# Row weights copied two blocks ahead, and the gather five blocks ahead asked for in front of a block's add

## The reference, cut to what matters

```python
top_i, top_w = route(h2, w_router, router_bias)          # 8 of 64 experts per token, and 8 weights
# assignments sorted by expert, each expert's rows padded to blocks of 128 rows
def block(args):
    tok, e = args
    return swiglu(h_pad[tok], w_gate[e], w_up[e], w_down[e])   # (silu(x@Wg) * (x@Wu)) @ Wd, 1024 -> 256 -> 1024
out = lax.map(block, (row_tok.reshape(n_blocks, 128), blk_exp))
out = out.reshape(n_rows, D) * row_w[:, None]
ffn = segment_sum(out, row_tok, num_segments=T + 1)[:T] + swiglu(h2, w_sh_gate, w_sh_up, w_sh_down)
x = x + g2 * ffn                                          # then a final RMSNorm
```

## Time and profile before

| | |
|---|---|
| median of 3 runs | 2043.7 us |
| the profiled execution's own time | 2044.4 us |
| its span | 2042.8 us |
| granted TensorE clock, mean of the span | 0.974 |
| PE, PEld, DVE, ACT, POOL busy | 93%, 75%, 57%, 47%, 19% |
| DMA, all queues | 399.63 MB, mean 196 GB/s |
| expert stage (first to last L2130 group) | 1084.85 to 1990.42 us |

### The profile page before, as it was taken

One profiled execution on the slowest core, in us unless ns is written; L12 is line 12 of the kernel. 1 busy time (PEld: TensorE's weight loads), 2 busy tenths in 40 slices (PEclk: granted clock), 3 DMA queues, 4 the chain that ended last, 5 costly groups with the idle time before them and its releaser, 6 DMA issues. The chain is left out here.

```text
span 2042.8 us, 37459 instructions
## 1 busy us (share of the span) xinstructions
PE 1904.9 (93%) x10449; PEld 1527.9 (75%) x10450; DVE 1159.4 (57%) x1715; ACT 967.4 (47%) x1395; POOL 385.4 (19%) x335
## 2 busy tenths in 40 slices
PE   4999999899899999988789999999999999999995
PEld 3999999899788666765547777777777777777772
DVE  4213401166438334555426777777777777777775
ACT  5110111244213222211246777777777777777773
POOL 0110100111111000000112223232233222323330
PEclk9999999899899999999889999999999999999998
DMA  7211321111343666325058997998998889898964
GB/s 261 74 48 45 115 60 31 31 64 62 134 143 123 230 217 220 134 94 197 1 205 275 304 350 205 324 313 285 336 312 273 268 271 308 234 347 263 298 193 176
DMA packets 181813, 399.63 MB, mean 196 GB/s; under 512 B 22137, under 2 KB 86897, under 8 KB 181758
## 3 DMA queue, kind: packets, MB, share of 16 engines
q1 hardware_dynamic: 149166, 312.16, 42.8%
q0 software_dynamic: 31392, 82.49, 15.7%
q10 hardware_dynamic: 1200, 4.26, 0.6%
HBM read 350.16 MB, written 80.64 MB: 211 GB/s over the span
## 5 line engine op out<-in xcount | busy, mean ns | idle before, releaser
L2214 DVE TENSOR_TENSOR wexp_lo<-wexp,wexp_hi 128x2048 fp32r<-128x2048 f32 x189 | 432.5, 2289 | 92.3 <-ACT wexp_hi L2156 70.8
L2156 ACT ACTIVATE wexp_hi<-wexp 128x2048 fp32r x190 | 362.0, 1907 | 47.5 <-issue 44.9
L2099 PE MATMUL bank<-wexp_hi,x_hi 128*128 128x512 f32 x744 | 301.0, 405 | 3.8 <-DVE wexp_lo L2214 3.8
L2099 PE MATMUL bank<-wexp_hi,x_lo 128*128 128x512 f32 x744 | 292.5, 393 | 0.0
L2099 PE MATMUL bank<-wexp_lo,x_hi 128*128 128x512 f32 x744 | 291.3, 391 | 0.0
L2070 POOL DMA_INDIRECT acc_d<-ob,ixs x92 | 168.4, 1831 | 606.6 <-DMA acc_d<-ob,ixs 377.1
L548 PE MATMUL bank<-hT_hi,w_hi 128*128 128x344 f32 x576 | 187.5, 325 | 7.3 <-DVEq L660 7.3
L548 PE MATMUL bank<-hT_hi,w_lo 128*128 128x344 f32 x576 | 185.3, 322 | 0.0
L548 PE MATMUL bank<-hT_lo,w_hi 128*128 128x344 f32 x576 | 184.7, 321 | 0.0
L2130 PE MATMUL bank<-wexp_down,hTe 128*128 x368 | 172.7, 591 | 0.0
L2099 PEld LDWEIGHTS bank<-wexp_hi,x_lo 128*128 128x128 f32 x744 | 140.7, 189 | 31.4
(11 more groups left out here) (369 smaller groups left out, 3444.6 us busy)
## 6 DMA issues: line engine op xcount, KB each, us to landing
wexp<-in_w_exp_gate SPq DMA_DIRECT2D x128, 512.0 KB, 9.1
wexp<-in_w_exp_up SPq DMA_DIRECT2D x128, 512.0 KB, 10.7
wexp_down<-in_w_exp_down SPq DMA_DIRECT2D x128, 512.0 KB, 10.1
wada<-in_w_ada SPq DMA_DIRECT2D x12, 2048.0 KB, 10.7
w_raw<-in_w_in SPq DMA_DIRECT2D x44, 512.0 KB, 3.9
gates_d<-gst POOLq DMA_DIRECT2D x48, 172.0 KB, 2.1
gate<-gates_d SPq DMA_DIRECT2D x16, 516.0 KB, 5.8
xn<-in_x_prompt ACTq DMA_DIRECT2D x8, 512.0 KB, 8.1
```

The costliest lines, as they stand in the source:

```text
L2099: last = pe.matmul(banks[0][:].rearrange("p (g n) -> p g n", g=2), stat[:, b, k, :], mov[:, b, :, k * FF:(k + 1) * FF], start=(k == 0 and ...
L2156: act.activation(w_hi[:, b, g, :], wexp[:, bass.ds(e & (RING - 1), 1), g, :].rearrange("p a n -> p (a n)"), ACT.Copy).then_inc(whi_ok, 1)
L2214: dve.tensor_tensor(w_lo[:, b, g, :], wexp[:, bass.ds(e & (RING - 1), 1), g, :].rearrange("p a n -> p (a n)"), w_hi[:, b, g, :], ALU.subtr ...
```

## The change

The table gets one more entry (`AHEAD` 5). GpSimd's body of block i asks for the gather of block i+5 where it asked for i+4, and therefore waits for one more turn and one more weight column (`x_tp` and `wc_ok` at i+4). The order gather, then add, in the body stays. VectorE copies the weight column of block i+2 at the start of body i, where it copied that of block i+3 behind `ixs`. So that the gather in the last body can start, TensorE and VectorE each raise their semaphore once more after their loops.

```diff
-AHEAD = 4
+AHEAD = 5
@@ gpsimd
                 for j in range(ROOMS, AHEAD):
                     pool.wait_ge(x_tp, j - 1)
                     pool.wait_ge(wc_ok, j - 1)
-                    gather(j, j)
+                    if j >= RING:
+                        pool.wait_ge(ix_ok, j - 3)
+                    gather(j, j % RING)
                 def block_of(i, q):
                     b = q % 2
-                    pool.wait_ge(x_tp, i + 3)
-                    pool.wait_ge(wc_ok, i + 3)
-                    pool.wait_ge(ix_ok, i + 1)
+                    pool.wait_ge(x_tp, i + 4)
+                    pool.wait_ge(wc_ok, i + 4)
+                    pool.wait_ge(ix_ok, i + 2)
                     pool.sem_inc(passed, 1)
                     gather(i + AHEAD, (q + AHEAD) % RING)
                     pool.wait_ge(ob_ok, 2 * i + 4)
@@ tensor
                 n = blocks_done(pe)
+                pe.wait_ge(xlo_ok, n * 2 + 4)
+                pe.sem_inc(x_tp, 1)
                 pe.wait_ge(wlo_ok, n * 2 + 5)
@@ vector
                 take(1, 1)
+                to_gather(4, 0)
...
-                e = entry(dve, 2, 1, E - 1)
-                weight(e, 2, 16)
-                rest_of_weights(e, 2, 0, 0)
+                rest_of_weights(entry(dve, 2, 1, E - 1), 2, 0, 0)
                 def block_of(i, q):
                     b = q % 2
                     to_gather(i + AHEAD, (q + AHEAD) % RING)
-                    rest_of_weights(entry(dve, i + 2, 1, E - 1), i + 2, b, 1)
+                    e = entry(dve, i + 2, 1, E - 1)
+                    weight(e, (q + 2) % RING, gathered(i, q, 2))
+                    rest_of_weights(e, i + 2, b, 1)
...
                     to_add(i, b)
-                    e = entry(dve, i + 3, 1, E - 1)
-                    weight(e, (q + 3) % RING, gathered(i, q, 3))
-                    rest_of_weights(e, i + 3, 1 - b, 0)
+                    rest_of_weights(entry(dve, i + 3, 1, E - 1), i + 3, 1 - b, 0)
                     rest_of_down(entry(dve, i + 1, 1, E - 1), i + 1)
...
                 blocks(dve, block_of)
+                n = blocks_done(dve)
+                for q in range(RING):
+                    dve.wait_ge(gat[q], 16 * ((n + 3 + RING - 1 - q) // RING))
+                    dve.sem_inc(passed, 1)
+                dve.sem_inc(wc_ok, 1)
```

## The result

The changed kernel took 2064.43 us (median of 4 runs, 2061.53 to 2066.59) beside 2043.43 us for the kernel before (2042.63 to 2046.57). The ratio is 1.0095, with the 95% interval [1.008, 1.0111]: slower, by 19 us by the ratio and 21 us by the medians. The forecast was 2057 us, with a range of 2042 to 2080. The profiled execution took 2064.94 us, its span is 2063.3 us.

What follows compares the result with a forecast made beforehand. TensorE was taken to bound the expert stage, busy 197.2 of 200 us. Terms -12 + 3.3 + 14.5 + 7.5 = +13.3 on 2044.4 gave 2057.7, forecast as 2057 us; range 2042 to 2080 for 8 in 10.

Steps and rivals of the forecast that it cites:

- A: Expert stage: earlier gathers no longer delay VectorE's weight column and thereby TensorE; 0 to 14.8 us gained, 12 taken.
- B: VectorE behind the 11 branches to a new span: the column joins the queue, 0.3 us each, +3.3 us.
- C: GpSimd's adds start at +8.8 instead of +7.53, behind stretched gathers; +14.5 us, kept between 1 and 23.
- D: End: the last add waits for an unused gather and starts 10.4 us later; +7.5 us, bounds 5 and 10.4.
- The third rival: Gathers start earlier but are stretched, only 2 us won; if TensorE still finds them late, 6 us gained, 2063; chance 0.08.
- Its sign: For B: VectorE's idle time behind a span's branch goes to 1.02 plus 0.3 us, in two pieces.
- the signs that were named: For C: most gathers last 2 us or more, adds start at +8.8 or later, VectorE waits at `ixs` in tens of blocks.
- a chain of landings that drifts against a margin: Successive first blocks of experts: each add waits for the landing before, drifting 0.76 us against 2.0 us margin; 14.5 us.
- The adds' delay is absorbed: Rival: adds start at +8.8 but the 2.2 us margin holds; 2044, no change, or faster; chance 0.20.
- Gather and add compete in the queue: Rival: gather packets precede the add's, landings get 0.7 us longer or more; 2066 to 2092; chance 0.18 above 2066.
- Its cover: End: TensorE's 16 matmuls hide 3.2 us of the last add's 10.4 us delay, leaving +7.2 on the path.
- PE after its idle time: End: after 7 us of idleness TensorE may run its next matmuls slower; a reason for the bounds 5 and 10.4.

Runs made afterwards that it cites:

- e5: e2 with the last body's gather, for a block that doesn't exist, left out: 2037.49 us, ratio 0.996.
- e2: Changed kernel with the weight column copied at its old place, three blocks ahead; only GpSimd's order is new: 2041.93 us, ratio 0.998.
- e1: Kernel before with only VectorE's weight column moved, two blocks ahead in front of the up weights; GpSimd as before: 2046.94 us, ratio 1.0005.
- e6: e1 with the weight column copied behind the up weights' low part instead of in front: 2042.93 us, ratio 0.9991.
- e9: Changed kernel with the gather five blocks ahead placed behind the block's add instead of in front: 2045.47 us, ratio 1.0008.
- e11: e7 with the gather placed behind the block's add instead of in front: 2043.03 us, ratio 0.9992.
- e12: e2 with four extra table-entry loads on GpSimd before the add's wait for the landing before, so adds start later: 2055.22 us, ratio 1.0046.
- e3: Changed kernel with the last body's gather, for a block that doesn't exist, left out: 2053.53 us, ratio 1.0041.
- e8: e2 with three extra table-entry loads on GpSimd before the add's wait for the landing before, so adds start later: 2050.54 us, ratio 1.0027.
- e7: Changed kernel with the weight column copied behind the up weights' low part instead of in front: 2111.07 us, ratio 1.0323.

## Why the forecast held, term by term

| term | forecast | measured | from |
|---|---|---|---|
| A, gathers earlier | -12 | -8 | e5 (-8.2 with the end nearly as before); profiled stage -7.6 in e2, -5.0 in e5; PE's waits for `xg`, -7.0 |
| B, column behind branches | +3.3 | +3 | e1 less e6, e9 less e11 |
| C, later adds | +14.5 | +13 to +15 | what is left of the total, so the sum closes by itself; 10.5 in the stage by e12 |
| D, the end | +7.5 | +11 | e3 (ratios, good to 4 us); +9.6 in the profile |
| sum | +13.3 | +19 to +21 | the result |

The direction was right, and so were the mechanisms of B, C and D; that of A was not. 7 us are missing, and they come from two terms, A and D.

**A** was right that late gathers cost PE time and wrong on the road. The prediction said that a late column "does harm by one road only: it delays `wexp_lo`". It hardly does: e1 cured it and gained nothing. The harm came by PE's own turn, which waited for `xg` six times, 7.0 us, with the block of 14.1 us among them. That row of the waits I left out of the argument, though it stood in the view beside the one I used; it would have bounded A near 7 instead of 14.8. The third rival named this road ("If PE's own turn still finds it late"), with A at 6 and 2063 us, and that is nearest to what was measured. But it had a chance of 0.08, and its reason, a gather that isn't really earlier, isn't what happened: PE finds none late any more. What I gave as its sign (the wait at the column falls below 10) came true and proved nothing, for the same reason: the column had been moved away from it.

**B** had the right size with the wrong count. Its sign came: behind a span's branch DVE is idle 1.03 us in front of the column and 0.17 in front of `wexp_lo`, which starts 1.51 us behind `ix` instead of 1.18 (medians of 11). Of this 0.33 a quarter of a microsecond reaches the beat at 11 span branches, and as much at the inner loop's. At face value the beats give 5.4 us; the two pairs of ratios give 3 each, each of them good to some 3 us.

**C** came in where it was put, and by the signs that were named: gathers of 2.2 us, 76 of 92 adds at +8.8 or later, 41 waits at `ixs`. Its model was a chain of landings that drifts against a margin. The runs support the margin (`ixs` comes more than 0.3 us behind the mark in 10 blocks of e2, with adds at +7.6, in 22 of e8, 26 of e12 and 35 of the changed kernel), and they add what it lacked, the loop through column and gather. PE's waits before the down product, +16.6 us, hold B and C together, for which I had 17.8. The agreement of 14.5 with 13 to 15 is partly luck: some 5 us of it seem to belong to the loop, which the model hadn't, and later adds alone bring 10.5. Of the 50.0 us at `ixs` 24.7 are for adds right behind their gather and 24.4 for adds that waited for the landing before. The rival "The adds' delay is absorbed" fell by e8 and e12. "Gather and add compete in the queue" fell too: landings went from 9.4 to 9.7 us, not by the 0.7 that it needed.

**D** was right to the place: the last add 17.82 us behind the mark, forecast 17.6. Its cover was right as well: DVE's first product comes 10.7 us later relative to the mark, PE's matmuls on it 7.7 later. What was mis-sized is named in the prediction as a bound: PE after its idle time. Windows of the changed kernel (us, busy of PE, PEld, DVE, ACT, POOL, granted clock, DMA share, GB/s):

```profile
2022.00:2030.00 8.00, 0.30 (x1) 0.00 (x0) 0.98 (x1) 0.00 (x0) 0.00 (x0) 0.84 0.51 166
2030.00:2033.00 3.00, 2.70 (x3) 1.18 (x4) 2.84 (x4) 0.00 (x0) 0.00 (x0) 0.50 1.03 422
2033.00:2037.00 4.00, 2.92 (x6) 1.06 (x4) 1.05 (x1) 2.85 (x7) 0.00 (x0) 0.85 1.02 413
```

Behind 8.00 us of idleness the granted clock is 0.50, the lower level of 1.2 GHz, and the eight matmuls take 5.62 us instead of 3.60: 2.0 us on the path, which with 7.7 makes the 9.6 of the profile, to a tenth.

## What to carry to other kernels

A wait is a loss only if taking it away moves the engine that bounds: before pricing one, look at what the same engine waits for next, and price first the bounding engine's own waits. Where a transfer is asked for in front of another on an in-order queue, follow the first one's conditions round: here the gather's needed an instruction that stood behind a wait for the second's landing. Undoing the order alone gave back 18 us in the changed kernel and 68 in e7, more than the 8 that the earlier gather is worth. "n blocks ahead" in the source says little; write down the sequence that the queue sees, and look at what the last iteration waits for. The edit that pays here is e5: gathers one add earlier, the column where it was, and no gather for a block that isn't there, 0.4% faster than the kernel before.

## What the runs showed of the hardware

- An indirect DMA on GpSimd that starts inside a `wexp_lo` of VectorE is stretched beyond the end of that instruction. Of the changed kernel's gathers 90 of 92 end 0.92 to 0.93 us behind it, and take 2.2 us in the median, against 1.05 in e7, where they start behind it. Adds (1.58 us alone) end 1.45 behind it, 53 of them in the kernel before. I expected the stretch; what it costs by itself no run isolates, but e7, whose gathers aren't stretched, is the slowest kernel.
- A table load in front of an instruction on VectorE shows as 0.92 us of idle time (median of 86 in e2). Where a DMA lands meanwhile, the idle time is put down to the DMA: 18 of the 49 gaps of the earlier trace rows are no longer than 1.01 us. 29 are longer than 1.15 us, which no gap of e2 is, and there the gather was late.
- The same idle time of TensorE was followed by either level of the clock: behind 3.07 us of idleness four matmuls took 1.98 us in the kernel before, at a granted clock of 1.00, and 3.50 us in e3, at 0.54.
